# RWKV inverse of a decoder trunk: b·r products, transpositions of b and k and z0 placed later, 14 gate products taken from the tail

## The reference, cut to what matters

```python
def token_mixer(h, w_in, ...):
    p = h @ w_in
    p_r, p_m, p_g = split(p)
    y_r = rwkv7_branch(p_r, ...) @ branch_w_rwkv
    y_m = mlstm_branch(p_m, ...) @ branch_w_mlstm
    g_r, g_m = split(sigmoid(p_g))            # 2 x 1024 gate channels
    return (g_r * y_r + g_m * y_m) @ w_out

def step(s, inp):                             # RWKV, 8 heads of 64, per token
    r_t, w_t, k_t, v_t, a_t, b_t = inp
    sa = einsum('bhvk,bhk->bhv', s, a_t)
    s = s * w_t + sa * b_t + v_t * k_t
    return s, einsum('bhvk,bhk->bhv', s, r_t)
```

## Time and profile before

| | |
|---|---|
| median of 3 runs | 1416.62 us (1415.69 to 1419.91) |
| the profiled execution's own time | 1416.96 us |
| its span in the profile | 1415.1 us |
| PE busy | 98% of the span |
| DVE, ACT, POOL busy | 73%, 20%, 5% |
| mean granted clock of PE | 0.996 |

### The profile page before, as it was taken

How to read it: one execution, slowest core, us unless ns; L and a number is a source line. 1 busy time by engine, 2 the same in 40 slices (tenths; PEclk the granted TensorE clock), 3 DMA queues, 4 the chain that set the end, 5 groups by cost and what they waited for, 6 DMA issues and landing times.

```text
span 1415.1 us, 30467 instructions
## 1 busy us (share of the span) xinstructions
PE 1389.4 (98%) x13536; PEld 1307.3 (92%) x13536; DVE 1028.0 (73%) x1718; ACT 288.2 (20%) x556; POOL 68.1 (5%) x137
## 2 busy tenths in 40 slices
PE   7999999999999999999999999999998999999998
PEld 3999999888888999999999999988997889999998
DVE  5899889788533769997988886787963355856665
ACT  2211101442231031110031110034332202211101
POOL 5110000000000000100000000000000000000000
PEclk9999999999999999999999999999999999999999
DMA  9999786443333658887768886454442257456540
GB/s 348 321 329 326 286 306 179 140 134 105 91 81 133 233 182 269 278 305 289 249 202 262 277 274 231 162 154 149 120 108 74 63 182 263 134 196 208 191 138 30
DMA packets 214050, 283.10 MB, mean 200 GB/s; under 512 B 13288, under 2 KB 177504, under 8 KB 213920
## 3 DMA queue, kind: packets, MB, share of 16 engines
q1 hardware_dynamic: 194976, 211.11, 46.2%
q0 software_dynamic: 17952, 69.21, 13.9%
q10 hardware_dynamic: 992, 0.85, 0.2%
HBM read 280.10 MB, written 1.05 MB: 199 GB/s over the span
## 4 chain that ended last, share of the span: by engine, by line
PE 95%; DVE 2%; issue 1%; DMA 1%; POOL 0%; ACT 0%; ACTq 0%; POOLq 0%; DVEq 0%
PE ps L1834 94%; PE ps L1838 1%; DMA ada_stage<-in_ada_w_dram 1%; DVE ada_acc L1046 1%; PE ps L2333 0%; DVE ada_turn L1052 0%; DVE ada_red L1053 0%; DVE arena L1275 0%; DVE arena L1278 0%; DVE arena L1276 0%; DVE hT L1819 0%; POOL ada_stage L613 0%; ACT xn L696 0%; ACT hT L696 0%; DVE x L1219 0%
## 5 line engine op out<-in xcount | busy, mean ns | idle before, releaser
L1834 PE MATMUL ps<-hT,ring 128*128 128x128 f32 (+2 forms) x2448 | 396.9, 319 | 1.3 <-ACT hT L696 1.3
L1834 PEld LDWEIGHTS ps<-hT,ring 128*128 128x128 f32 (+1 forms) x2448 | 351.7, 191 | 36.1 <-issue 8.6
L1834 PE MATMUL ps<-y_both,arena 128*128 128x128 f32 x2304 | 266.6, 275 | 1.0 <-issue 1.0
L1834 PEld LDWEIGHTS ps<-y_both,arena 128*128 128x128 f32 x2304 | 261.8, 192 | 1.5 <-issue 1.5
L1834 PE MATMUL ps<-arena 32*32 32x32 f32 (+6 forms) x4368 | 204.3, 230 | 8.5 <-issue 8.1
L1834 PEld LDWEIGHTS ps<-arena 32*32 32x32 f32 (+3 forms) x4368 | 193.3, 138 | 18.9 <-issue 16.1
L1834 PE MATMUL ps<-arena,ring 128*128 128x128 f32 (+1 forms) x1312 | 186.5, 294 | 0.0
L1834 PEld LDWEIGHTS ps<-arena,ring 128*128 128x128 f32 x1312 | 171.3, 192 | 6.6
L1046 DVE SCALAR_TENSOR_TENSOR ada_acc<-ada_stage,cond,ada_acc 128x1024 f32<-128x1024 f32 (+1 forms) x119 | 148.9, 1251 | 5.7 <-DMA ada_stage<-in_ada_w_dram 1.8
L1834 PE MATMUL ps<-y_both,ring 128*128 128x128 f32 (+1 forms) x1024 | 150.8, 301 | 0.0
L1834 PEld LDWEIGHTS ps<-y_both,ring 128*128 128x128 f32 x1024 | 138.7, 192 | 6.5
(11 more groups left out here) (317 smaller groups left out, 1342.3 us busy)
## 6 DMA issues: line engine op xcount, KB each, us to landing
ring<-in_ffn_w_in_dram SPq DMA_DIRECT2D x86, 1024.0 KB, 7.8
ada_stage<-in_ada_w_dram POOLq DMA_DIRECT2D x66, 1024.0 KB, 5.6
ring<-in_ffn_w_out_dram SPq DMA_DIRECT2D x44, 1024.0 KB, 6.2
ring<-in_mix_w_in_dram SPq DMA_DIRECT2D x46, 512.0 KB, 5.2
ring<-in_mix_w_in_dram SPq DMA_DIRECT2D x12, 1024.0 KB, 5.7
ring<-in_mix_w_in_dram SPq DMA_DIRECT2D x6, 1536.0 KB, 6.5
ring<-in_mix_w_out_dram SPq DMA_DIRECT2D x8, 1024.0 KB, 5.0
arena<-in_ada_w_dram SPq DMA_DIRECT2D x6, 1024.0 KB, 13.6
```

Source lines behind the costliest of these rows:

```text
L1834: return nc.tensor.matmul(out_, lhsT, rhs, start=start, stop=stop, **kw)
```

## The change

- `mrb` on PE is moved from behind `p2` to just before `uz`, after the gates of place h, with a wait for ACT's copy of `z0`. Its masks on DVE move behind `xf` and the diagonal tile.
- The first half of `products_mk` moves from behind `px 8` to behind `g32`, the second from behind `g32` to behind `g64`. The masks on DVE move with them.
- `turned b` moves from behind `x 8` to behind `x 32`, and `turned k` from there to behind `z0`; `z0` moves from behind `g64` to behind `xo`. ACT's copies move with them, and PE's waits for these copies are renamed.
- 14 gate products leave the tail (27 to 13): n gets 1 more, a 2, b 1, c 2, d 2, e 3, f, g and h 1 each.

No instruction is added or removed.

```diff
--- before.py
+++ after.py
@@ -135,8 +135,8 @@
 
 
 
-GATE_PLACES = (("num", 5), ("n", 6), ("a", 6), ("b", 6), ("c", 5), ("d", 6), ("e", 5), ("f", 6), ("g", 5), ("h", 5),
-               ("i", 4), ("j", 5), ("k", 5), ("tail", 27))
+GATE_PLACES = (("num", 5), ("n", 7), ("a", 8), ("b", 7), ("c", 7), ("d", 8), ("e", 8), ("f", 7), ("g", 6), ("h", 6),
+               ("i", 4), ("j", 5), ("k", 5), ("tail", 13))
 GATE_BANK = (2, 3, 6, 7, 6, 7, 6, 7)
 
 
@@ -965,22 +965,22 @@
                 gates("b")
                 power("px 8")
                 gates("c")
-                turned("b")
                 gates("d")
                 copied("g32", 3)
                 gates("e")
-                turned("k")
+                turned("b")
                 gates("f")
                 copied("g64", 3)
-                for h in range(2):
-                    ac.wait_ge(*PE.at(l, "z0"))
-                    act(az[:, h::2, 64:128], view(ps[:, 4 + h, :], 8, 64), ACT.Copy, "z0" if h else None)
                 for g in range(2):
                     ac.wait_ge(*PE.at(l, "turned a"))
                     act(az[:, 8 * g:8 * g + 8, 0:64], view(ps[:, g, :], 8, 64), ACT.Copy, "turned a" if g else None)
                 gates("g")
                 ac.wait_ge(*PE.at(l, "xo"))
                 act(xf[0:32, :, 32:64], view(ps[0:32, 2, :], 16, 32), ACT.Copy, "xo")
+                for h in range(2):
+                    ac.wait_ge(*PE.at(l, "z0"))
+                    act(az[:, h::2, 64:128], view(ps[:, 4 + h, :], 8, 64), ACT.Copy, "z0" if h else None)
+                turned("k")
                 gates("h")
                 for n, bank in ((0, 3), (1, 2)):
                     ac.wait_ge(*PE.at(l, f"uz {n}"))
@@ -1687,30 +1687,30 @@
                 masked(o32, "o32", 1)
                 dv.wait_ge(*AC.at(l, "p2"))
                 flipped("p2t", pt, px[:, 0])
-                dv.wait_ge(*PE.at(l, "mrb"))
-                for h in range(2):
-                    free(V.tensor_tensor(mrb[:, h::2, :], view(ps[:, 4 + h, :], 8, 64),
-                                         mask_t[:, 0, :].unsqueeze(1).broadcast_to([P, 8, 64]), ALU.mult),
-                         "mrb" if h else None)
                 power("px 4")
                 power("px 8")
-                masked_mk(0)
                 grow("x 8", px[:, 1])
                 dv.wait_ge(*DV.last(l))
                 flipped("x16", xt, px[:, 1])
-                masked_mk(1)
+                masked_mk(0)
                 grow("x 32", xt)
                 dv.wait_ge(*DV.last(l))
                 flipped("x64", pt, xt)
                 for r in range(4):
                     rows, at = slice(32 * r, 32 * r + 32), 32 * (r % 2)
                     free(V.tensor_copy(xf[rows, :, at:at + 32], xt[rows, :, :]))
+                masked_mk(1)
                 dv.wait_ge(*PE.at(l, "xo"))
                 free(V.tensor_copy(xf[64:96, :, 32:64], view(ps[64:96, 2, :], 16, 32)), "xf")
                 free(V.tensor_tensor(view(diag.rearrange("p a b -> p (a b)"), 4, 2, 64),
                                      ident2[:, :].unsqueeze(1).unsqueeze(1).broadcast_to([P, 4, 2, 64]),
                                      view(pend[:, :, :].rearrange("p g c -> p (g c)"), 4, 4)[:, :, 1:3].unsqueeze(3)
                                      .broadcast_to([P, 4, 2, 64]), ALU.mult))
+                dv.wait_ge(*PE.at(l, "mrb"))
+                for h in range(2):
+                    free(V.tensor_tensor(mrb[:, h::2, :], view(ps[:, 4 + h, :], 8, 64),
+                                         mask_t[:, 0, :].unsqueeze(1).broadcast_to([P, 8, 64]), ALU.mult),
+                         "mrb" if h else None)
                 for n, bank in ((0, 1), (1, 0)):
                     dv.wait_ge(*PE.at(l, f"uz {n}"))
                     free(V.tensor_copy(uz[:, 8 * n + 1:8 * n + 8:2, :], quad(bank)), f"uz {n}")
@@ -2373,14 +2373,6 @@
                 pe.wait_ge(*DV.at(l, "nt16"))
                 pe.wait_ge(*DV.at(l, "gates 1"))
                 blocks("p2", 2, pt, px[:, 0])
-                pe.wait_ge(*DV.at(l, "y_m"))
-                for q, t, h, hh in heads:
-                    ar, bt, kt, hats = sets[q // 2]
-                    at = 64 * (2 * q + t)
-                    for c in range(2):
-                        last = mm(ps[home(c, h), 4 + h, at:at + 64], bt[hh, q % 2, t * P + 64 * c:t * P + 64 * c + 64],
-                                  ar[hh, q % 2, t, 1, chunks[c]])
-                last.then_inc(*PE.step("mrb"))
                 gates("a")
                 pe.wait_ge(*DV.at(l, "p2t"))
                 power("px 4")
@@ -2389,23 +2381,19 @@
                 gates("b")
                 pe.wait_ge(*DV.at(l, "px 4 turned"))
                 power("px 8")
-                pe.wait_ge(*DV.at(l, "mrb"))
-                products_mk(0)
                 gates("c")
                 pe.wait_ge(*DV.at(l, "px 8 turned"))
                 blocks("x 8", 2, pt, px[:, 1])
-                pe.wait_ge(*AC.at(l, "turned v"))
-                turned("b")
                 gates("d")
                 pe.wait_ge(*DV.at(l, "x16"))
                 blocks("g32", 3, o32, xt)
-                pe.wait_ge(*DV.at(l, "kr 0"))
-                products_mk(1)
+                pe.wait_ge(*DV.at(l, "y_m"))
+                products_mk(0)
                 gates("e")
                 pe.wait_ge(*AC.at(l, "g32"))
                 blocks("x 32", 2, px[:, 1], px[:, 0])
-                pe.wait_ge(*AC.at(l, "turned b"))
-                turned("k")
+                pe.wait_ge(*AC.at(l, "turned v"))
+                turned("b")
                 gates("f")
                 pe.wait_ge(*DV.at(l, "x 32"))
                 for i in range(16):
@@ -2413,13 +2401,9 @@
                         last = mm(ps[quarter[2 * c], 3, 32 * i:32 * i + 32], o64[quarter[2 * c + 1], i, :],
                                   xt[quarter[2 * c + 1], i, :])
                 last.then_inc(*PE.step("g64"))
-                pe.wait_ge(*DV.at(l, "kr 1"))
-                for q, t, h, hh in heads:
-                    i, at = 4 * q + 2 * t + h, 64 * (2 * q + t)
-                    for c in range(2):
-                        last = mm(ps[chunks[c], 4 + h, at:at + 64], mk[home(c, h), i, 0:64], v_tm[home(c, h), q, t, hh])
-                last.then_inc(*PE.step("z0"))
-                pe.wait_ge(*AC.at(l, "turned k"))
+                pe.wait_ge(*DV.at(l, "kr 0"))
+                products_mk(1)
+                pe.wait_ge(*AC.at(l, "turned b"))
                 for q in range(4):
                     for t in range(TT):
                         at = P * (2 * (q % 2) + t)
@@ -2433,11 +2417,27 @@
                         last = mm(ps[quarter[2 * c], 2, 32 * i:32 * i + 32], pt[quarter[2 * c], i, :],
                                   px[quarter[2 * c], 0, i, :])
                 last.then_inc(*PE.step("xo"))
+                pe.wait_ge(*DV.at(l, "kr 1"))
+                for q, t, h, hh in heads:
+                    i, at = 4 * q + 2 * t + h, 64 * (2 * q + t)
+                    for c in range(2):
+                        last = mm(ps[chunks[c], 4 + h, at:at + 64], mk[home(c, h), i, 0:64], v_tm[home(c, h), q, t, hh])
+                last.then_inc(*PE.step("z0"))
+                pe.wait_ge(*AC.at(l, "turned a"))
+                turned("k")
                 gates("h")
+                pe.wait_ge(*AC.at(l, "z0"))
+                for q, t, h, hh in heads:
+                    ar, bt, kt, hats = sets[q // 2]
+                    at = 64 * (2 * q + t)
+                    for c in range(2):
+                        last = mm(ps[home(c, h), 4 + h, at:at + 64], bt[hh, q % 2, t * P + 64 * c:t * P + 64 * c + 64],
+                                  ar[hh, q % 2, t, 1, chunks[c]])
+                last.then_inc(*PE.step("mrb"))
                 pe.wait_ge(*PO.at(None, f"xf {l}"))
                 pe.wait_ge(*DV.at(l, "xf"))
                 pe.wait_ge(*AC.at(l, "xo"))
-                pe.wait_ge(*AC.at(l, "turned a"))
+                pe.wait_ge(*AC.at(l, "turned k"))
                 for n, banks in enumerate(((3, 1), (2, 0))):
                     for e in range(4 * n, 4 * n + 4):
                         at = e % 4 * P
```

## The result

The changed kernel took 1407.48 us (median of 4 runs, 1406.04 to 1409.21); the kernel before 1416.97 us beside it. The ratio is 0.9931, 95% interval 0.9911 to 0.995: 9.5 us or 0.7% less, where 7.6 us were forecast. A second set of 6 runs gave 1406.58 us and 0.9932 (0.9914 to 0.995). The profiled execution of the first set took 1406.04 us, with a span of 1404.0 us against 1415.1.

What follows compares the result with a forecast made beforehand. PE, busy for 98% of the span, was taken to bound the kernel; 3.6 us won in layer 0 and 4.3 in layer 1, together 7.9 off 1416.96, gave 1409.1, predicted as 1409.0 us; range 1405.5 to 1413.0, chance 0.8.

Steps and rivals of the forecast that it cites:

- The reading of the gaps: PE's inverse gaps are waits for the next 256-instruction block; entries at least 3.45 us apart (layer 1: 3.75), shorter blocks stall.
- Rival (e): Gaps belong to the products and travel with mrb; only 0.8 us won, from place n, 1416.2 us; chance 0.03.
- mrb out of its place: Behind p2, eight gates of place a replace mrb and fill its long gap: 1.9 us won in layer 0, 2.0 in layer 1.
- the clock: Without 2 us of idle behind short products, the granted clock stays up after p2: 1.7 us won per layer.
- The end of px 4: New stall where a block boundary falls 11 instructions before px 4's end: 0.8 us taken, between 0.3 and 2.3.
- Within g32: Boundary within g32, behind 8 gates: only a late fetch stalls it, 0.2 us taken, between 0 and 1.
- The boundary behind x 32: Boundary at the end of turned b, after only 1.7 us of work: stall of 1.3 us taken, between 0.1 and 3.3.
- The dependences and the tail: Waits on ACT and DVE are covered by gates, and the tail with 13 products still hides the head norm: no cost.
- (f): The queue reads ahead enough to cover the new boundaries; 10 to 12 us go, 1405 to 1407 us; chance 0.11.
- (b): The clock falls once more, behind x 32 and turned b: one fall 1410.7 us, two 1412.4; chance 0.15.
- (c): Loads delay the three block fetches; stalls gain 2 to 4 us per layer, 1413 to 1417 us; chance 0.12.
- (d): Slower: the stall behind x 32 reaches 3.3 us and the clock falls there in both layers, 1420 us; chance 0.03.

Runs made afterwards that it cites:

- Experiments 1 and 2: Two follow-ups: before_pad (kernel before, 1416.73 us in one execution) tested whether gaps follow blocks or products; p2_nine (changed kernel, 1435.7 us) tested the time floor per block.
- p2_nine: Changed kernel with the 64 products of p2 made nine times in layer 0, 2048 instructions more; the execution took 1435.7 us.
- moves_only: Changed kernel with the new order of products but the old numbers of gate products (27 in the tail); 1407.94 us, ratio 0.9947.
- after_again: Second set of runs of the changed kernel itself, nothing altered, with its own profile; 1406.58 us, ratio 0.9932.
- spread_more: Changed kernel with nine more gate products taken from the tail (13 to 4), one more in each of a to i; 1416.07 us, ratio 0.9993.
- a_nine: Changed kernel with one more gate product in place a (9) and one less in the tail (12); 1409.72 us, ratio 0.9946.
- spread_hold: spread_more with the DMAs of the second and later branch weights waiting until PE has done the y products; 1406.81 us, ratio 0.9931.
- mrb_only: Kernel before with mrb alone, and its masks, moved ahead of uz, all other products in place; 1414.57 us, ratio 0.9987.
- experiment 4: Fewer products in the tail than in the changed kernel: spread_more (1416.07 us), then spread_hold (1406.81 us) with branch-weight loads held.
- mrb_back: Changed kernel with mrb alone, and its masks, put back behind p2; 1415.42 us, ratio 0.999.
- gates_only: Kernel before, old order, with the new numbers of gate products (13 in the tail); 1415.34 us, ratio 0.9998.
- before_pad: Kernel before with 8 of the 64 products of n made twice in each layer, 32 instructions more per layer; one execution took 1416.73 us.

## Why the prediction was right, step by step

**The reading of the gaps** held. Experiments 1 and 2 show both halves of it, that they follow the blocks and that a block takes 3.45 us at least. The rule of the Trainium skill that was weighed there ("Runtime: NRT & Kernel Launch", section "Instruction fetch mechanics"), that the fetch is hidden, does not hold for runs of such short products: p2_nine shows a gap in every block. Rival (e) is out.

**One more gate product in n** (0.4 us a layer): no gap ahead of p2 in either layer, while moves_only, without it, shows 0.38 us there in layer 0. Right.

**mrb out of its place** (1.9 and 2.0 us) and **the clock** (1.7 us a layer): both gaps gone, clock 1.00. Right in size. The two stretches without their gaps shrank by 1.5 and 2.4 us (1.4 and 2.2 in after_again), where the clock had been given 1.7 each. One trace of the gap in layer 0 can stay: after_again has 0.29 us within the gates of a. The text gave the place of mrb to "the gates of place a, and eight of them"; moves_only has six and shows no gap there either. The count of products at a place did little: with the moves alone the median is within 1.4 us of both sets of the whole change.

**The end of px 4** (0.8 us): 0.37 us in layer 0 and 0.66 us in layer 1, there four transpositions before the end of turned v; in after_again 1.20 and 1.02 us. The size is right between executions, and the two executions point to what decides it. Timeline of after_again, and its queues from 382.9 to 384.0 and from 384.0 to 385.1 us:

```profile
381.90 1.46 PE L1834 MATMUL ps<-hT,ring 128*128 128x256 f32 x6 [0.29 <-issue]
...
386.45 0.31 PE L1834 MATMUL ps<-arena 32*32 32x64 f32 x6 [1.20 <-issue]
```

```profile
q1 hardware_dynamic: 496, 0.25, 90.1%
...
q8 instruction: 1, 0.02, 5.6%
```

The block was entered at 381.90, but while product 48's loads ran no instruction packet came until 384.0, 2.1 us behind the entry and not 1.1. In the first profile this packet (384.4) came just ahead of the bulk of these loads, and the gap is 0.37. **Within g32** (0.2 us): 0.28 and 0.46, in after_again 0.53 and 0.52.

**The boundary behind x 32** (1.3 us) was mis-sized: it is 0 in both layers and both profiles, and the gap of 1 to 1.5 us that was to show at the end of turned b is not there. In layer 0 the step that failed is how far ahead of PE the sequencer asks for a block: half of the four gate products in front, 0.8 us, was taken. In the changed kernel's DMA slices (403.0 to 404.3, then 405.9 to 408.9) the packets of the last two blocks stand:

```profile
DMA  0000009000000000000000000000000000000000
...
DMA  0000000000700000000000000000007899833597
```

They begin at 403.20 and near 406.65. The first comes 1.1 us behind the gap's end at 402.12. If the second too comes 1.1 us behind the sequencer's entry, that entry was at 405.6, when PE was in the gates that end at 407.50; its first product of that block comes 14 matmuls into x 32, at 407.6. By this estimate the sequencer was 2.0 us ahead, and the 1.8 us that were missing were covered. The packet also came 1.5 us ahead of product 80's loads (the digits from 408.15 on), so they added nothing; where they came first, in spread_more, this boundary stalled 1.77 us.

In layer 1 the term was put at a place where no boundary lies. The forecast took the boundaries of layer 0 for both layers, but the earlier trace rows had the long gap 31 matmuls into mrb and not 13. So all boundaries of layer 1 lie 18 matmuls later, and this one falls behind the gates of f, at the start of g64. The block ahead of it holds most of x 32, turned b and seven gate products, 4.8 us (1087.9 to 1092.7): nothing to stall. a_nine, whose boundaries lie 4 instructions off, has small gaps at both places and so shows them, layer 0 in turned b and layer 1 one matmul before the end of the gates of f:

```profile
408.55 0.34 PE L2333 MATMUL ps<-ident,ring 64*128 64x64 f32 x5 [0.52 <-issue]
...
1095.20 0.38 PE L1834 MATMUL ps<-hT,ring 128*128 128x256 f32 x1 [0.46 <-issue]
```

This one term, twice 1.3 us, is nearly the whole of the difference between the 7.9 us of the sum and the 10.7 us of the first profile. The other way went a gap near the end of the y products of layer 1, 0.74 and in after_again 0.92 us, not foreseen. In after_again the gaps left add up to 4.5 us, where the sum had 4.6, and the gain is 8.5 us: there the stalls of px 4, g32 and y happen to make up for the missing one. That the sum comes so near is in part luck.

**The dependences and the tail** at nothing: right; no wait on DVE or ACT has taken the place of a gap. spread_hold has a tail of 4 products and is as fast.

**The rivals.** (f), the queue reads ahead enough to cover the new boundaries, came true at one of them, behind x 32 in layer 0, and not at px 4 and g32; the 9.5 us measured lie between the forecast and its 10 to 12. (b), the clock falls behind x 32, did not come in the changed kernel but did in mrb_only, behind a gap of 1.90 us. (c), late fetches, is real: experiment 4 shows packets held back by loads and three gaps that shrank by 5.7 us without them. In the changed kernel it acts only in small, at the end of px 4 (0.37 against 1.20 us); at the thin block behind x 32 the packet came ahead of the loads in both profiles. (d) did not come; at its place, behind x 32, spread_more stalled for 1.77 us, with no fall of the clock.

## What to carry to other kernels

Where gaps of PE are put down to "issue", count the instructions between them; distances of 128 matmuls or a multiple, as here, point to a short supply of instructions. Then what counts is the work in each block of 256 instructions, in program order. Spread short products between long ones, check every later boundary too, since each moved product shifts them all, and keep large loads away from the moment when a thin block is fetched. A part of such a change cannot be judged alone: here the parts gave 1.0, 1.8 and 8.4 us, and the whole 9.5.

## What the runs showed of the hardware that was not expected

- The floor per 256 instructions is the same with the clock at 1.2 GHz (3.45 or 3.73 us, p2_nine) and at 2.4 GHz (3.45 and 3.75 us).
- In spread_more three instruction packets came only as loads in flight ended, and PE stood up to 2.92 us. A DMA wait that changes no product (spread_hold) took 9.3 us off the median, more than any one part of the change did (8.4); 5.7 us of it are seen in these three gaps.
- The clock fell behind gaps of 1.90, 1.99, 2.10, 2.17 and 2.45 us (p2_nine, at 382.12) that follow short products, once behind one of 1.48 us (a_nine, layer 1), but not behind those of 1.82 (mrb_back, gates_only, layer 1) and 1.84 us (before_pad and mrb_only, layer 0), nor of 1.85 us in spread_hold, nor in spread_more behind 2.16 and 2.92 us. The length of the gap alone does not decide; what does was not tried.
- The stretch between the inverses took 606.09 to 606.14 us in all fourteen profiles. The inverses themselves scatter: two profiles of the changed kernel differ by 1.5 us in layer 0 and 0.75 in layer 1, so a smaller effect there cannot be read from single profiles. The places of the gaps can.
